# Identity products on TensorE during row norms and column splits of a two-block network

## What is computed

```python
def rmsnorm(x, g):
    x32 = x.astype(jnp.float32)
    y = x32 * lax.rsqrt(jnp.mean(x32 * x32, axis=-1, keepdims=True) + EPS)
    return (y * g.astype(jnp.float32)).astype(x.dtype)

x = x + 0.5 * swiglu(rms_norm(x, ffn1_norm[l]), ffn1_w_gu[l], ffn1_w_down[l])
x = x + hybrid_mixer(rms_norm(x, mix_norm[l]), ...)
x = x + 0.5 * swiglu(rms_norm(x, ffn2_norm[l]), ffn2_w_gu[l], ffn2_w_down[l])
```

## Time and profile before

| | |
|---|---|
| Median of 3 runs | 5232.81 us (5229.2 to 5236.91) |
| Profiled execution | 5234.47 us, its span 5232.6 us |
| TensorE products | 4592.9 us busy, 88% of the span |
| TensorE weight loads | 3871.5 us, 74% |
| VectorE | 3090.2 us, 59% |
| ScalarE | 2284.1 us, 44% |
| Mean granted TensorE clock | 0.937 of full speed |
| DMA | 827.30 MB, mean 158 GB/s |

### The profile page before, as it was taken

How to read it: one execution, slowest core, us unless ns; L and a number is a source line. 1 busy time by engine, 2 the same in 40 slices (tenths; PEclk the granted TensorE clock), 3 DMA queues, 4 the chain that set the end, 5 groups by cost and what they waited for, 6 DMA issues and landing times. The chain is left out here.

```text
span 5232.6 us, 72620 instructions
## 1 busy us (share of the span) xinstructions
PE 4592.9 (88%) x25788; PEld 3871.5 (74%) x25788; DVE 3090.2 (59%) x7252; ACT 2284.1 (44%) x4332; POOL 6.3 (0%) x20
## 2 busy tenths in 40 slices
PE   7778899999999999786699999959787798887788
PEld 2446788888888888664699977759775697786677
DVE  7545687555544444424688766656466655547655
ACT  6424333566633333222446855534334444444444
POOL 0000000000000000000000000000000000000000
PEclk9889999999999999887899999979898899999989
DMA  8401444555576666311477788835332454343343
GB/s 305 157 27 33 135 122 136 156 179 180 188 218 183 185 185 188 95 65 33 145 206 228 251 261 256 266 123 190 120 113 78 171 190 144 131 155 101 121 160 146
DMA packets 380091, 827.30 MB, mean 158 GB/s; under 512 B 31912, under 2 KB 189736, under 8 KB 362132
## 3 DMA queue, kind: packets, MB, share of 16 engines
q1 hardware_dynamic: 379800, 823.58, 49.3%
HBM read 713.25 MB, written 110.20 MB: 157 GB/s over the span
## 5 line engine op out<-in xcount | busy, mean ns | idle before, releaser
L170 DVE TENSOR_TENSOR w_low__6<-w_raw,w_high__6 128x512 fp32r<-128x512 f32 x544 | 362.2, 688 | 441.1 <-ACT w_high__6 L165 440.8
L158 PE MATMUL hidden<-hT_high,w_high__6 128*128 128x512 f32 x1152 | 456.7, 396 | 15.8 <-DVE w_low__6 L170 15.8
L160 PE MATMUL hidden<-hT_high,w_low__6 128*128 128x512 f32 x1152 | 450.7, 391 | 0.0
L159 PE MATMUL hidden<-hT_low,w_high__6 128*128 128x512 f32 x1152 | 449.0, 390 | 0.0
L170 DVE TENSOR_TENSOR w_low__11<-w_raw__2,w_high__11 128x512 fp32r<-128x512 f32 x544 | 362.6, 689 | 122.7 <-ACT w_high__11 L165 107.5
L165 ACT ACTIVATE w_high__6<-w_raw 128x512 fp32r<-128x512 f32 x544 | 324.3, 624 | 215.3 <-PE side L160 204.4
L165 ACT ACTIVATE w_high__11<-w_raw__2 128x512 fp32r<-128x512 f32 x544 | 321.8, 624 | 71.8 <-DMA w_raw__2<-in_peer_v 32.5
L158 PE MATMUL hidden__3<-hT_high__2,w_high__11 128*128 128x256 f32 x1152 | 331.7, 288 | 11.6 <-DVE w_low__11 L170 11.6
L160 PE MATMUL hidden__3<-hT_high__2,w_low__11 128*128 128x256 f32 x1152 | 327.3, 284 | 0.0
L159 PE MATMUL hidden__3<-hT_low__2,w_high__11 128*128 128x256 f32 x1152 | 327.1, 284 | 0.0
L158 PEld LDWEIGHTS hidden<-hT_high,w_high__6 128*128 128x128 f32 x1152 | 217.0, 188 | 58.6 <-DVE w_low__6 L170 16.0
(11 more groups left out here) (1012 smaller groups left out, 12700.5 us busy)
## 6 DMA issues: line engine op xcount, KB each, us to landing
w_raw<-in_peer_u SPq DMA_DIRECT2D x128, 512.0 KB, 4.1
w_raw<-in_peer_v SPq DMA_DIRECT2D x128, 512.0 KB, 4.0
w_raw__2<-in_peer_u SPq DMA_DIRECT2D x128, 512.0 KB, 4.3
w_raw__2<-in_peer_v SPq DMA_DIRECT2D x128, 512.0 KB, 4.9
activated_dram<-activated SPq DMA_DIRECT2D x128, 256.0 KB, 4.4
routing_dram<-routing SPq DMA_DIRECT2D x32, 1024.0 KB, 6.5
routing_chunk<-routing_dram SPq DMA_DIRECT2D x16, 2048.0 KB, 10.8
activated_again<-activated_dram SPq DMA_DIRECT2D x128, 256.0 KB, 4.3
```

Source lines behind the costliest of these rows:

```text
L158: nc.tensor.matmul(out, lhs[0], rhs[0], start=start, stop=False, skip_group_check=True)
L159: nc.tensor.matmul(out, lhs[0], rhs[1], start=False, stop=False, skip_group_check=True)
L160: return nc.tensor.matmul(out, lhs[1], rhs[0], start=False, stop=stop, skip_group_check=True)
L170: return nc.vector.tensor_tensor(low, src, high.bitcast(F32), ALU.subtract)
```

## The change

`rms_rows` takes the identity as an optional argument, and `norm_cols` alone passes it. Where it is given, TensorE gets a list in that stage: 8 + 6n products of the identity with itself, n the number of tiles, so 32 for four tiles and 20 for two. `split_cols` gets 16 in each call. All write the first 128 columns of a PSUM bank of the stage, which nobody reads. They wait for nothing and nothing in the stage waits for them, except the meeting at its end.

```diff
-def rms_rows(nc, units, eps):
+def spin(nc, st, block, ident, times):
+
+
+    spun = st.psum("spun", [P, 512])
+
+    @block.tensor
+    def _(pe):
+        for _ in range(times):
+            nc.tensor.matmul(spun[:, 0:P], ident[:, :], ident[:, :], start=True, stop=True)
+
+
+def rms_rows(nc, units, eps, ident=None):
...
         block = st.begin()
+        if ident is not None:
+            spin(nc, st, block, ident, 8 + 6 * n)
...
-        rms_rows(nc, [(xs[:, t, :], xn[:, k, :], D) for k, t in enumerate(tiles)], EPS)
+        rms_rows(nc, [(xs[:, t, :], xn[:, k, :], D) for k, t in enumerate(tiles)], EPS, ident)
...
-def split_cols(nc, src, high, low):
+def split_cols(nc, ident, src, high, low):
...
         block = st.begin()
+        spin(nc, st, block, ident, 16)
...
-            split_cols(nc, hT, *h_parts)
+            split_cols(nc, ident, hT, *h_parts)
```

## The result

The changed kernel takes 5249.09 us (median of 10 runs, 5241.97 to 5255.18), the kernel before 5229.92 (10 runs, 5223.32 to 5238.76). The medians lie 19.2 us apart. The profiled execution took 5250.07 us.

What follows compares the result with a forecast made beforehand. TensorE, busy 88%, looked like the bound, with about 660 us at 1.2 GHz. Short splits 17.5 + long split 0.3 + two-tile norms 0.7 - turning stages 4.3 = +14.2 us on 5232.81: 5247 us, range 5235 to 5259.

Steps and rivals of the forecast that it cites:

- The cost of one product: Inserted fp32 products of 128x128: two records each, 0.22 us at full clock and 0.42 us at 1.2 GHz.
- How long the low clock lasts in a split: In the short splits' 16 products, w us at 1.2 GHz before full clock; mean 4.3, ends 3.0 and 5.7.
- For w = 4.3: With 4.3 us at the low clock, 16 products take 5.6 us, 20 take 6.5, 32 take 9.1.
- The long split: The one split of 512 columns: 6.2 us against 6.1, costing 0.3 us with the spread of w.
- The norms of two tiles: Seven row norms with 20 products each: 7.1 us against 7.2, taken as 0.1 us each, 0.7 in all.
- Norms of four tiles: Three row norms with 32 products each: 9.7 us against 10.8, hidden behind ScalarE and VectorE, cost 0.
- The turning stage: Transposes and copies out of PSUM behind each norm: a warm start saves about 0.43 us, ten times, 4.3.
- The first products: Next stage's products behind each split: no gain, as TensorE idles 4.9 to 7.4 us and the clock falls.
- The clock at the start of a split: Low as each short split begins, after over 3 us of idleness; the 2.5 us lateness, seven times, depended on it.
- the first rival: Clock stays full up to the split, whose products then take 4.2 us against 3.7; 5232 us, chance 0.10.
- The sum: Whole kernel: 17.5 + 0.3 + 0.7 - 4.3 = +14.2 us on the median of 5232.81, giving 5247 us.

Runs made afterwards that it cites:

- the moved kernel: Against the kernel before: norms' products kept, the splits' products moved to the start of TensorE's list in the stage behind; 5215.02 us, again 5219.94 us.

## Why the prediction was right

*The cost of one product: right.* In the inserted products a record follows the last by 0.112 us at full clock and 0.213 at the low one, so a product is 0.223 or 0.43 us. With 0.223n + 0.48w and 0.2 us for the last result, n and w (the time at 1.2 GHz) read from each stretch, all 18 stretches of inserted products come out within 0.04 us. One split of the table: 16 products, w = 3.1, gives 3.57 + 1.49 + 0.2 = 5.26; the two rows with 0.71 say 5.24 and 5.29. The Trainium skill, "TensorE: Matmul & The Clock Gate", section "Back-to-back issue gap", would put a product of 128 columns at 0.107 us on the low clock; here it takes twice that for each of two records. This case's trace decides: the page's figure is for bf16, and an fp32 product that is two records is to be priced by a row of fp32.

*How long the low clock lasts in a split: mis-sized.* "For w = 4.3" was read from the products behind the splits. In the short splits it measured 3.5 on average (by the table 4.7, 3.5, 3.4, 3.1, 3.1, 3.2, 3.5), and so a split takes 5.8 us instead of 6.2: +14.2 us for the seven, where the prediction had 17.5. It had bounded w by 3.0 and 5.7.

*The long split:* 6.0 us low, above the 5.7 of the prediction's bound, gave +0.9 instead of +0.3, in both traces. *The norms of two tiles:* two of seven were longer, +1.3 instead of +0.7. *Norms of four tiles:* 9.4 to 9.8 us of products under 10.8, hidden, as said.

*The turning stage:* 0.46 us each, -4.5 instead of -4.3. In the second trace one of the ten stayed at its old length.

*The first products:* nothing gained, as said. The gap behind the split was the place to decide it, and they begin at 0.50 eight times of eight, in both traces.

*The clock at the start of a split:* "this holds if the clock is low when the split begins" was too strict a condition. It was low in five of the eight, and in the other three it fell 0.8 to 1.1 us later, while the products ran; in the second trace it was still full at three and fell within 1.4 us. The low stretch then came all the same, so the first rival (4 us a split) is out: no short split took under 5.5. The transposes warmed the clock before the change and kept it at 1.00 after; that they don't count as activity (the Trainium skill, same page, "Part 4: PE-mode transpose") this case's trace doesn't bear out, though behind a warm norm it can't tell who kept it.

*The sum:* +14.2 was forecast; the touched stages give +11.9 and +12.3 in two traces, the runs +17.8 with 12.6 to 23.0, the spans of two traces after against three before +17.3. Some 5 us of the difference of spans lie outside the touched stages, where single executions scatter by as much: the kernel before alone spans 5225.6 to 5232.6. The runs say that not all of it is scatter, and the prediction has no term for it; its cause is open. That 5247 us stands only 2 us from the median of 5249 is partly luck. The splits were priced 3.3 us too high, the other stages lost some 5 us that were put at nothing, and the median of three runs from which the sum starts was 2.9 us above that of ten.

## What to carry to other kernels

Warming products ahead of a gap like these, with 5.1 to 7.7 us of idleness, cost their time and give nothing behind it; put them into the gap itself, into the list of the stage that waits for its loads, and let them end just before the data is there. Count them by their own price (here 0.22 us each at full clock, plus 0.48 us for each microsecond that the clock is low, in fp32) against the idle time of that very stage, and never where all engines meet behind them with less other work than that. Check the sum of the stages against many runs, for here the two differed by 5 us and more. And weigh a clock's mean with care: it rose in the slower kernel too.

## What the runs showed that was not expected

The low stretch at the same place isn't the same length each time: 3.0 to 6.1 us in the splits, 0 to 6.1 in the norms of two tiles, where two of seven met a clock that was still full and had all 20 products through in 4.70 us. Untouched stages differ between executions of one kernel by some us with it: the second `peer` took 884.7, 882.0 and 882.2 us in three traces of the kernel before. And the gain of warm starts, near what was expected in most stages, did not add up over the program: the two mixer chains of the moved kernel were longer than the mean before by 9.2, 6.0 and 3.4 us in its three traces. In the changed kernel and the one with 32 products in the splits the runs were likewise slower than the touched stages say. Why is open.
